# A decoder block with expert retrieval on one core: both tiles through attention ahead of the expert rows, and plain fp32 products for q, k and v

## The reference

```
mod = silu(c) @ w_ada + b_ada                     # six rows of 1024: shift, scale, gate, twice
h = rms_norm(x) * (1 + scale1) + shift1
z = h @ w_in                                      # q, k, v of 8 FoX heads; f; q, k, v of 8 MoBA heads; 2 gates of 1024
y_a = fox_attention(norm(q_a), norm(k_a), v_a, log_sigmoid(f + b))   # causal, logit + F[t] - F[s]
y_b = moba_attention(norm(q_b), norm(k_b), v_b)   # one block of 256: causal with ALiBi slopes
x = x + gate1 * ((sigmoid(g_a) * (y_a @ w_up_fox) + sigmoid(g_b) * (y_b @ w_up_moba)) @ w_out)
h2 = rms_norm(x) * (1 + scale2) + shift2
q = h2 @ w_peer_q                                 # 8 heads x 2 halves x 128
scores = q . sub_keys; 16 best of each half; 16 best of their sums; g = softmax of these 16
x = x + gate2 * sum over 128 experts of g * gelu(h2 . u[e]) * v[e]
```

## Time and profile before

| | |
|---|---|
| time, three runs | 1014.5, 1017.3, 1018.57 us; median 1017.3 |
| the profiled execution | 1019.0 us, its span 1017.2 us, mean granted clock of TensorE 0.943 |
| busy: TensorE, VectorE, ScalarE, GpSimd | 841.0, 649.5, 362.3, 288.1 us |
| expert rows fetched | 268.45 MB, the transfers' share 65.2% of the span |
| weights and other inputs | 82.89 MB, 23.1%; of them 16 late transfers of 1 MB |
| largest groups | TensorE ps_y L1415 491.4 us, VectorE dots L869 307.7 us, VectorE w_lo L554 54.4 us, ScalarE w_hi L956 47.9 us |

### The profile page before, as it was taken

One profiled execution on the slowest core, in us unless ns is written; L12 is line 12 of the kernel. 1 busy time (PEld: TensorE's weight loads), 2 busy tenths in 40 slices (PEclk: granted clock), 3 DMA queues, 4 the chain that ended last, 5 costly groups with the idle time before them and its releaser, 6 DMA issues.

```text
span 1017.2 us, 9145 instructions
## 1 busy us (share of the span) xinstructions
PE 841.0 (83%) x2764; PEld 470.4 (46%) x2764; DVE 649.5 (64%) x1612; ACT 362.3 (36%) x1015; POOL 288.1 (28%) x275
## 2 busy tenths in 40 slices
PE   4889889998978888878987975988698777777776
PEld 4767656657943333333434533653263332222222
DVE  4799957723868587777543643975778644455444
ACT  2456434532235545654221231341233222222221
POOL 3000000000223334424422531335245343333330
PEclk9999979998998899979998987999899899999999
DMA  9958845547779699978999997999989999999995
GB/s 318 384 204 311 313 168 191 207 152 265 273 309 421 253 373 377 420 283 342 419 411 400 400 410 265 379 418 409 422 338 423 392 423 422 422 420 422 421 422 238
DMA packets 84872, 351.95 MB, mean 346 GB/s; under 512 B 6668, under 2 KB 19028, under 8 KB 52056
## 3 DMA queue, kind: packets, MB, share of 16 engines
q0 software_dynamic: 36864, 268.45, 65.2%
q1 hardware_dynamic: 46264, 82.89, 23.1%
q10 hardware_dynamic: 1696, 0.04, 0.1%
HBM read 350.31 MB, written 1.05 MB: 345 GB/s over the span
## 4 chain that ended last, share of the span: by engine, by line
PE 43%; DMA 27%; DVE 21%; issue 4%; ACT 3%; POOL 1%; ACTq 1%; SPq 1%; POOLq 0%; DVEq 0%
PE ps_y L1415 18%; DMA ring<-in_peer_uv,eid 15%; DVE ring L869 6%; DMA late_ring<-in_w_peer_q 4%; DMA out_y<-wide 3%; DMA late_ring<-in_w_out 3%; PE bank L1355 3%; PE bank L1364 2%; DMA late_ring<-in_w_up_moba 2%; PE bank L1380 2%; PE ps_y L1226 2%; PE bank L1226 2%; PE ps_y L1227 2%; PE ps_y L1228 2%; PE bank L1227 2%
## 5 line engine op out<-in xcount | busy, mean ns | idle before, releaser
L1415 PE MATMUL ps_y<-ring,diag 128*128 128x512 f32 x1024 | 491.4, 629 | 114.2 <-ACT diag L1130 112.9
L493 POOL DMA_INDIRECT ring<-in_peer_uv,eid x256 | 278.5, 1088 | 690.0 <-PE ps_y L1415 416.8
L869 DVE CUSTOM_DVE_ANT_0 ring<-ring,gates 128x1024 f32<-128x1024 f32 x256 | 307.7, 1224 | 183.8 <-DMA ring<-in_peer_uv,eid 182.7
L1415 PEld LDWEIGHTS ps_y<-ring,diag 128*128 128x128 f32 x1024 | 197.2, 200 | 382.9 <-issue 211.5
L1119 ACT ACTIVATE gel<-adot 128x2 f32<-128x2 f32 x128 | 26.0, 203 | 394.3 <-DVE adot L869 394.1
L1130 ACT ACTIVATE diag<-ident,ew 128x128 f32<-128x128 f32 x256 | 86.7, 386 | 0.0
L1123 ACT ACTIVATE ew<-g_sb,gel 128x1 f32<-128x1 f32 x256 | 61.5, 287 | 4.2
L956 ACT ACTIVATE w_hi<-ring 128x512 fp32r<-128x512 f32 x80 | 47.9, 626 | 29.5 <-PE bank L1228 28.1
L554 DVE TENSOR_TENSOR w_lo<-ring,w_hi 128x512 fp32r<-128x512 f32 x80 | 54.4, 690 | 4.4 <-PE ps_y L1228 1.9
L1226 PE MATMUL bank<-w_hi,hT_hi 128*128 128x512 f32 x96 | 40.4, 421 | 7.0 <-DVE w_lo L554 4.0
L1380 PE MATMUL bank<-tT,late_ring 128*128 128x128 f32 x256 | 31.6, 284 | 12.7 <-DMA late_ring<-in_w_peer_q 12.7
(11 more groups left out here) (184 smaller groups left out, 859.8 us busy)
## 6 DMA issues: line engine op xcount, KB each, us to landing
ring<-in_w_ada SPq DMA_DIRECT2D x12, 2048.0 KB, 9.0
ring<-in_w_in SPq DMA_DIRECT2D x10, 2048.0 KB, 8.0
ring<-in_w_peer_q SPq DMA_DIRECT2D x4, 2048.0 KB, 8.1
late_ring<-in_w_peer_q SPq DMA_DIRECT2D x8, 1024.0 KB, 21.8
ring<-in_w_out SPq DMA_DIRECT2D x2, 2048.0 KB, 10.8
ring<-in_peer_uv,eid POOLq DMA_INDIRECT x256
late_ring<-in_w_out SPq DMA_DIRECT2D x4, 1024.0 KB, 17.5
ring<-in_w_up_fox SPq DMA_DIRECT2D x1, 2048.0 KB, 9.1
```

What stands on the lines that cost most here:

```text
L493: pool.indirect_dma_start(uv_row(n), None, peer_uv, bass.IndirectOffsetOnAxis(ap=eid[:, n:n + 1], axis=0)).then_inc(s_uv[n % NP], 16)
L869: dve.tensor_tensor_reduce(u_row(n), u_row(n), h2[:, n // P, :], 1.0, 0.0, ALU.mult, ALU.add, adot[:, at:at + 1]).then_inc(s_dot, 1)
L1415: ins = pe.matmul(ps_y[:, cut], diag[:, n % ND, :], v_row(n)[:, cut], start=first, stop=last)
```

## The change

- Tile 1 passes attention, up and out ahead of the expert rows too: four attention groups with the same 32 gate blocks over 44 steps, then up, out and norm2 of both. What stays behind the rows is tile 1's h2T and 14 of the 16 queries (slots 1 to 25), and the choices (slots 0 to 58). Each weight is loaded once; `late_ring` is gone.
- q, k, v and f are plain fp32 products; only the gate projections keep the split in three, and hT is split behind VA.
- The forget gates are computed behind the norms of KA, `f` stands behind VA.
- Small inputs come in one tensor; weights are laid out in 2 MB tiles by the host, the sub-keys already turned.
- Rows are fetched into 12 buffers that come free one by one: six at first, two from row 26, two from row 40, two from row 54 (`BUFFERS`, `await_first_use`).

```diff
+BUFFERS = [("V", 0), ("E", 0), ("R3a", 0), ("R3b", 0), ("R0a", 0), ("R0b", 0),
+           ("R2a", 26), ("R2b", 27), ("R1a", 40), ("R1b", 41), ("Ka", 54), ("Kb", 55)]
 SLOT = {
-    "queries0": (0, 1),
-    "attention": [2 + 3 * n // 2 for n in range(2 * STEPS)],
-    "up": (35, 36, 39, 40), "up_dve": (36, 37, 40, 41),
-    "mix": (40, 42),
-    "out": (43, 44, 47, 48), "out_dve": (44, 45, 48, 49),
-    "norm2": 50, "h2T": 51,
-    "queries1": (52, 53, 56, 57, 62, 63, 74, 75),
-    "keys": ((None, None, 2, 13, 24), (54, 59, 69, 78)),
-    "pairs": ((None, None, 4, 15, 26), (55, 61, 71, 80)),
-    "experts": ((None, None, 6, 17, 28), (56, 62, 73, 82)),
+    "h2T1": 0,
+    "queries": ((None, None, 1, 2, 7, 8, 14, 15), (4, 5, 10, 11, 17, 18, 24, 25)),
+    "keys": ((None, 0, 4, 10, 18), (30, 38, 46, 54)),
+    "pairs": ((None, 1, 6, 12, 20), (32, 40, 48, 56)),
+    "experts": ((None, 2, 8, 14, 22), (34, 42, 50, 58)),
 }
...
+def plan_buffers():
+    order, waiting = [], list(BUFFERS)
+    fills, last, table = {}, {}, []
+    for n in range(ROWS):
+        while waiting and waiting[0][1] <= n:
+            order.insert(0, waiting.pop(0)[0]) if n else order.append(waiting.pop(0)[0])
+        name = order.pop(0)
+        order.append(name)
+        table.append((name, fills.get(name, 0), last.get(name)))
...
+        def await_first_use(eng, name):
+            if name == "V":
+                await_item(eng, ("y", 1, 1, 3))
+            elif name == "E":
+                await_block(eng, NGATE * KD - 1)
+            elif name[0] == "K":
+                await_item(eng, ("qp", 1, 7))
+            else:
+                await_item(eng, {"0": ("o", 1, 1), "1": ("qp", 1, 5), "2": ("qp", 1, 3), "3": ("up", 1, 1, 1)}[name[1]])
...
+        peer_place = [K_chunk, ring[:, 2, :, :], ring[:, 1, :, :], K_chunk]
...
+            await_block(sp, NGATE * KD - 1)
+            sp.dma_start(skT[:], keys_t).then_inc(s_keys, 16)
+            await_item(sp, ("S", 1, 1, HEADS - 1))
+            sp.dma_start(peer_place[0], peer_t[0]).then_inc(s_peer[0], 16)
+            await_item(sp, ("up", 1, 1, 0))
+            sp.dma_start(peer_place[1], peer_t[1]).then_inc(s_peer[1], 16)
+            await_item(sp, ("o", 1, 3))
+            sp.dma_start(peer_place[2], peer_t[2]).then_inc(s_peer[2], 16)
+            await_item(sp, ("qp", 1, 1))
+            sp.dma_start(peer_place[3], peer_t[3]).then_inc(s_peer[3], 16)
...
             for c_ in range(NZ_QKV):                                # VectorE
-                    low_parts(j, j + 1)
...
-                if c_ == QA:
+                if c_ == KA:
                     forget_gates()
...
-            attention(0, 0)                                         # VectorE
-            attention(0, 1)
+            for t in range(TILES):
+                for g in range(2):
+                    attention(t, g)
             await_item(dve, ("ada", ADA - 1))
-            for n in range(4):
-                up(0, n // 2, n % 2)
+            for c_ in range(2):
+                up(0, c_)
+            up(1, 0)
             norm2_scale()
             for n in range(4):
                 out_part(0, n)
             norm2(0)
-            for n in range(2):
-                choose_keys(0, n)
-                choose_pairs(0, n)
-                choose_experts(0, n)
+            up(1, 1)
+            choose_keys(0, 0)
+            choose_pairs(0, 0)
+            choose_experts(0, 0)
+            for n in range(4):
+                out_part(1, n)
+            norm2(1)
...
                     for k in range(KD):                             # TensorE, q, k and v
-                        z_block(key[1], k, places, s_item)
+                        for t in range(TILES):
+                            ins = pe.matmul(spots[t], hT[:, k, t * P:(t + 1) * P], w[:, k, :],
+                                            start=(k == 0), stop=(k == KD - 1))
...
+            for t in range(TILES):                                  # TensorE
+                for g in range(2):
+                    attention(t, g)
             for n in range(4):
                 up(0, n // 2, n % 2)
+            up(1, 0, 0)
             turn_wide(0, 0)
+            turn_wide(0, 1)
+            up(1, 0, 1)
             norm2_rows()
             for n in range(4):
                 out_part(0, n)
+            for g in range(2):
+                up(1, 1, g)
             turn_h2(0)
-            for m in range(Q_FIRST):
+            for m in range(2):
                 queries(0, m)
+            for h in range(2):
+                turn_wide(1, h)
+            for n in range(4):
+                out_part(1, n)
```

More of the change, by code:

```diff
@@ L73, in lay, with scored, z_order @@
 def lay(behind, slot, stage):
     behind.setdefault(slot, []).append(stage)
-def lay_attention(behind, attention):
-    for n, slot in enumerate(SLOT["attention"]):
-        lay(behind, slot, lambda n=n: attention(1, n // STEPS, range(n % STEPS, n % STEPS + 1)))
+def scored(t, m):
+    if t == 0 and m < 2:
+        return [m]
+    return [m - 1, m] if m % 2 == 1 else []
+def z_order(tiles):
+    items = []
+    behind = []
+    for c in range(NZ_QKV):
+        items += [("z", c, t) for t in range(tiles)]
+        items += behind
+        if c == VA:
+            items.append("f")
+        behind = [("qkT", c, t) for t in range(tiles)] if c in QK else []
+        if c == KA:
+            items.append("Fcol")
+        if c:
+            items.append(("ada", ADA_FIRST + c - 1))
+    return items + behind + [("ada", ADA_FIRST + NZ_QKV - 1)]
@@ new lines, in psum_plan, with gate_blocks, block_kernel @@
+    for t in range(tiles):
+        later += [(slot, 1, query_items(t, m)) for m, slot in enumerate(SLOT["queries"][t]) if slot is not None]
+    for _, _, keys in sorted(later, key=lambda entry: entry[:2]):
+        items += keys
+    return {key: n for n, key in enumerate(items)}
+def gate_blocks(u):
+    total = NGATE * 8
+    return range(u * total // ALL_STEPS, (u + 1) * total // ALL_STEPS)
+def block_kernel(nc, x, small, b_ada, b_fgate, ada_t, in_t, up_t, out_t, peer_t, keys_t, peer_uv, out):
@@ L546, in low_parts @@
             def low_parts(first, last):
-                for j in range(first, last):
+                for j in range(first, min(last, NGATE * KD)):
                     n, k = j // KD, j % KD
@@ L1093, in choice @@
                 act.activation(gt, gt, ACT.Exp).then_inc(s_g1, 1)
-            behind = {}
-            for m in range(Q_FIRST, 8):
-                lay(behind, SLOT["queries0"][m - Q_FIRST], lambda m=m: queries(0, m))
-            lay_attention(behind, attention)
-            for h in range(2):
-                lay(behind, SLOT["mix"][h], lambda h=h: to_tT(1, "mixT", h))
-                lay(behind, SLOT["h2T"], lambda h=h: to_tT(1, "h2T", h))
-            lay(behind, SLOT["norm2"], norm2_root)
-            for m in range(8):
-                lay(behind, SLOT["queries1"][m], lambda m=m: queries(1, m))
-            for t in range(TILES):
-                for n in range(0 if t else 2, len(GROUPS[t])):
-                    lay(behind, SLOT["experts"][t][n], lambda t=t, n=n: choice(t, n))
-            def run(slot):
-                for stage in behind.get(slot, ()):
-                    stage()
             def expert_weights(pair):
@@ L1131, in expert_weights, with run @@
                                    scale=ew[:, c_:c_ + 1]).then_inc(s_diag, 1)
-            attention(0, 0)
-            attention(0, 1)
-            norm2_diagonals()
+            behind = {}
+            for t in range(TILES):
+                for n in range(0 if t else 1, len(GROUPS[t])):
+                    lay(behind, SLOT["experts"][t][n], lambda t=t, n=n: choice(t, n))
+            for h in range(2):
+                lay(behind, SLOT["h2T1"], lambda h=h: to_tT(1, "h2T", h))
+            for t in range(TILES):
+                for m, slot in enumerate(SLOT["queries"][t]):
+                    if slot is not None:
+                        lay(behind, slot, lambda t=t, m=m: queries(t, m))
+            def run(slot):
+                for stage in behind.get(slot, ()):
+                    stage()
+            for t in range(TILES):
+                for g in range(2):
+                    attention(t, g)
             sigmoids(0)
+            sigmoids(1)
             for h in range(2):
                 to_tT(0, "mixT", h)
-            sigmoids(1)
+            norm2_diagonals()
             norm2_root()
```

637 lines of the change are left out of this document (282 added, 355 removed).

## The result

The changed kernel takes **1040.7 us** (median of four, 1038.0 to 1042.7) where the kernel before takes 1015.9 beside it: 1.0255 of the time, 95% interval 1.0193 to 1.0318. It is 2.5% slower. I had forecast 1012: the time lies inside the range of 985 to 1043, but the sign is wrong. The profiled execution took 1041.1 us, its span is 1039.3, the mean granted clock 0.948.

What follows compares the result with a forecast made beforehand. Time was taken as the moment fetching can run freely, plus the rows left times 2.48 us, plus 10.5 us: 498 + 1.5 + 502 + 10.5 = span 1012, also 1012 on the median; range 985 to 1043.

Steps and rivals of the forecast that it cites:

- Step 1: The front, before the first plain product: small transfers and transposes leave, so the product starts at 37 us, before 47.3.
- step 2: q, k and v as 96 plain products, 82.4 us, with an 8.2 us wait for Fcol: sum 108, end at 145.
- 0.92 of the other reading: q, k and v: true FP32 as four passes of 0.23 us per product, giving 88 us, 6 more.
- Step 3: Attention of both tiles with the gate projections: 106 us, between 102 and 141, end at 251.
- 6 of the other reading: Low clock behind the wait for Fcol: by the skill's rule it costs 6 us, where the forecast takes 2.
- Steps 4 and 5: From attention's end: first fetch at +61.8 us (313), first pair of rows on TensorE at +79.2 (330).
- Step 6: Crowded pairs to slot 25: TensorE binds with 150 us of work; with waits and half clock 168, ending at 498.
- Step 7: From row 54's fetch at 498: never waits again, 202 rows in 502 us, plus 1.5 and 10.5; span 1012.
- A: Crowded pairs and attention: TensorE's queue is never starved and no attention step waits; span 989; chance 0.27.
- B: Attention paced by a round trip of 3.2 us a step through VectorE and ScalarE, 141 us: 1047; chance 0.17.
- C: Crowded pairs run as badly as before, a factor of 1.32, 198 us, 30 more: 1042; chance 0.15.
- D: Whole kernel: the transfers saved come through in full, 40 us, with a fetch busy throughout: 977; chance 0.03.

Runs made afterwards that it cites:

- x2: Changed kernel with Fcol one chunk later, behind the product of QB instead of KA: 1031.3 us, ratio 1.0195 to the kernel before.
- x6: Changed kernel with all 32 gate blocks in tile 0's 22 attention steps and none in tile 1's: 1044.2 us, ratio 1.0268 to the kernel before.
- x1: Changed kernel with the late buffers joining at rows 28, 44 and 60 instead of 26, 40 and 54: 1014.0 us, 0.999 of the kernel before.
- x4: Changed kernel with the edits of x1 and x2, plus the first six gate roundings and four low parts made during the last v product: 998.1 us, ratio 0.9824.
- x7: x4 with tile 1's queries spread to slots 4 to 29 and late buffers joining at rows 32, 50 and 68: 997.1 us, ratio 0.9829.
- y2: Kernel before with tile 1's 22 attention steps all in slot 2 of the expert loop: 1038.6 us, ratio 1.0235.
- x5: Changed kernel with all six later buffers joining at row 60, six in use until then: 1035.2 us, ratio 1.0188 to the kernel before.

## Why the prediction was wrong, step by step

- **Step 1** (37) and **step 2** (end 145): measured 38.3 and 145.1. The plain product took 0.859 us (13.75 for 16) against 0.858 from the row of up and not the 0.92 of the other reading, and the hole for Fcol 7.6 us (86.65 to 94.25) against 8.2. The other side of that wait was visible too: x2 removes it for nothing.
- **Step 3** (attention, 106) is the first step that failed: 118.3, 12 us more. TensorE's own busy time of 108.5 at a mean clock of 0.93 is 100 us of work at full clock, 2 less than my 102. But it was idle for 9.9 us where I took 4, and the low clock cost some 8 us (7% of 118.4) where I took none. Nearly all of that is in tile 0's half: its 22 steps took 61.0 us at a mean clock of 0.86, tile 1's 57.4 at 1.00. (Between executions the same attention took 115.1 to 120.6, so the miss is 9 to 15.) I had written that the wait behind 138 to 150 "is not there in the new order"; another was: VectorE entered attention behind ScalarE's roundings, and the chain shows it at 146.22. The Trainium skill ("TensorE: Matmul & The Clock Gate", HAM oscillation) says that idle gaps bring the clock down. The trace agrees in attention (0.50 in 158 to 164, behind the holes between 146 and 152); for Fcol's hole it cost 2.6 us, nearer to my 2 than to the 6 of the other reading. Idle gaps are not the whole of it: in x6 the clock stayed at 0.50 for 46.4 us in which TensorE was busy 44.4, and there the measurement decides.
- **Steps 4 and 5** (+61.8 to the first fetch, +79.2 to the first pair on TensorE): +62.4 and +78.7 from the end of attention. Right, so their absolute times are off only by step 3.
- **Step 6** (the crowded pairs, 168) took 176. I had put down 150 us of work, waits of TensorE of 2.4 and 12 us, and 4 of low clock. TensorE was idle 18.7 of 176, 4 more than I had; 4.5 of it, between 393 and 405, stand ahead of any opening and had no term at all. Its 157.3 busy us at a mean clock of 0.91 are an estimated 143 of work, 7 less than my 150, and 14 of low clock, 10 more than my 4. So the waits were named and nearly right in size, and the term that was most mis-sized is the clock. The 14 us of waits I booked as given, without asking what it would take to avoid them, and x1 shows that much of them, and the 11 rows that went unfetched with them, stood on three numbers of a table.
- **Step 7** (498 and 514 to the end) was 518 and 521.3. The rate is as said, 422 GB/s, and the tail of 10.5 us too (1028.8 to 1039.3). The 7 us more lie between the issue of row 54 (517.07) and the last landing: 511.7 us for 202 rows, where 502 + 1.5 was my figure. The first three microseconds run at 240 GB/s and the next six below 400, and 1.4 MB beside the rows passes in that time (409 GB/s over 521.3 us is 213.2 MB; 202 rows are 211.8). That accounts for some 5; the rest stays open.

From milestone to milestone the misses are 0 (attention begins at 145.1), 12, minus 0.5, 8 and 7, together the 27 us between my span of 1012 and 1039.3. That x1 saves 26.7 us and so comes out near my 1012 is a coincidence: I had booked 14 us of those waits, and its attention was 15 us longer than mine. The rival cases: **A** is out (TensorE was starved). **B**'s price is out, since the steps took 2.7 us on the mean and tile 1's 2.6, not 3.2, but its place was right: TensorE's waits in attention are for VectorE. B's own 1047 lay outside my range, which ended at C. **C**, a factor of 1.32 on the crowded pairs, is out: it was 176 of 150, 1.17, and that C's 1042 comes near the measured time is luck. **D** is out. Misses of 12, 8 and 7 us, all on the slow side, did together what no rival did alone, and I gave "slower" 0.34 by whole rivals only. Of the change as a whole: the new order delays the first fetch by 57 us (268.74 to 325.84), and the undisturbed fetch behind it gives that much back only if rows keep coming while TensorE still computes queries. In x1 that balance is zero (0.999); with Fcol moved and the first gate blocks rounded earlier as well it is a gain of 1.8% (x4).

## What to carry to other kernels

When requests are issued in order, a wait placed on request n also holds every later one, so put the opening of a new buffer behind the row at which its release is surely past, and price that line in rows not fetched, not only in the engine's idle time. Before moving the filling out of a stage of small products, look at the granted clock as well as at idle time: a stage whose engine is busy all the time can still run at half speed (x6 against the changed kernel). Before crediting an edit with a few microseconds of one stage, look how much that stage differs between executions that the edit does not touch (118.6 against 112.5 us for the same attention in x4 and x7). When several terms of a sum can each only miss on one side, put their sum among the rivals.

## What the hardware showed that I had not expected

- Back-to-back small products (256 columns with 64 or 8 rows, 128x128 transposes) ran for 46.4 us at a granted clock of 0.50 with TensorE busy 44.4 (x6); the same in y2 at 300 to 324 us (0.50 and 0.51, busy 23.9 of 24).
- One and the same attention, 44 steps, took 115.1 to 120.6 us in the changed kernel, x1 and x5, at mean clocks of 0.93, 0.90 and 0.96.
- 202 fetches in a row with twelve buffers kept 416 to 423 GB/s in every slice but the last. Among the crowded pairs (342 to 518 us) six buffers (x5) made a mean of 323, and x1's six to ten, twelve from row 60 on, 378.
